# The experts' scatter as fp32r matmuls of a high and a low part

## The reference

```python
def moe_swiglu(h, w_router, w1, w3, w2):
    ...
    combine = jnp.sum(jax.nn.one_hot(top_idx, N_EXPERTS, dtype=jnp.float32)
                      * gate[..., None], axis=1)
    y = jnp.zeros(xt.shape, jnp.float32)
    for e in range(N_EXPERTS):
        y = y + combine[:, e:e + 1] * swiglu(xt, w1[e], w3[e], w2[e]).astype(jnp.float32)
```

## Time and profile before

| | us |
|---|---|
| median of 3 runs (1304.88 to 1309.19) | 1306.67 |
| the profiled execution, its own time | 1308.46 |
| its span, first to last instruction | 1306.3 |

### The profile page before, as it was taken

How to read it: one execution, slowest core, us unless ns; L and a number is a source line. 1 busy time by engine, 2 the same in 40 slices (tenths; PEclk the granted TensorE clock), 3 DMA queues, 4 the chain that set the end, 5 groups by cost and what they waited for, 6 DMA issues and landing times.

```text
span 1306.3 us, 29353 instructions
## 1 busy us (share of the span) xinstructions
PE 1275.3 (98%) x13943; PEld 723.1 (55%) x13943; DVE 314.3 (24%) x415; ACT 200.7 (15%) x278; POOL 50.4 (4%) x44
## 2 busy tenths in 40 slices
PE   8999999997999999999999999999999999999996
PEld 7888888896793355345335434533643553353354
DVE  5454444588431011010101101020110110100001
ACT  5344443354430000000000000000000000000001
POOL 2000000032010000000000000000000000000000
PEclk9999999997789999999999999999999999999998
DMA  9965555233167999999999999999999999999940
GB/s 347 393 213 189 183 181 189 95 118 131 56 226 295 394 409 403 386 406 411 388 398 414 384 402 410 413 397 387 415 390 401 409 405 386 399 411 395 381 188 34
DMA packets 97885, 419.04 MB, mean 321 GB/s; under 512 B 8585, under 2 KB 14770, under 8 KB 97762
## 3 DMA queue, kind: packets, MB, share of 16 engines
q1 hardware_dynamic: 94288, 410.59, 80.6%
q0 software_dynamic: 1808, 5.45, 1.6%
q10 hardware_dynamic: 1666, 1.10, 0.3%
HBM read 415.01 MB, written 2.10 MB: 319 GB/s over the span
## 4 chain that ended last, share of the span: by engine, by line
PE 93%; DVE 3%; ACT 1%; issue 1%; DMA 1%; POOL 0%; DVEq 0%; POOLq 0%
PE psum L670 44%; PE psum L681 22%; PE psum L589 7%; PE psum L591 7%; PE psum L590 7%; PE psum L597 2%; PE psum L661 2%; PE psum L786 1%; DVE rope_z L1319 1%; DVE low L1135 1%; PE psum L651 0%; PE psum L796 0%; PE psum L808 0%; DMA consts<-in_table 0%; ACT high L929 0%
## 5 line engine op out<-in xcount | busy, mean ns | idle before, releaser
L670 PE MATMUL psum<-up,xg 128*32 128x448 f32 x6144 | 580.2, 539 | 2.4 <-DVE xg L1216 2.4
L670 PEld LDWEIGHTS psum<-up,xg 128*32 128x32 f32 x6144 | 198.9, 110 | 376.2 <-issue 372.5
L681 PE MATMUL psum<-down,hid_t 128*32 128x256 f32 x5376 | 291.5, 379 | 0.0
L681 PEld LDWEIGHTS psum<-down,hid_t 128*32 128x32 f32 x5376 | 174.8, 110 | 117.9 <-issue 3.9
L1135 DVE TENSOR_TENSOR low<-raw,high 128x2048 fp32r<-128x2048 f32 x51 | 116.9, 2292 | 95.4 <-ACT high L929 95.3
L1255 DVE TENSOR_TENSOR sil<-sil,psum 128x1344 f32<-128x1344 f32 x16 | 24.9, 1554 | 472.3 <-PE psum L670 472.3
L929 ACT ACTIVATE high<-raw 128x2048 fp32r<-128x2048 f32 x51 | 97.9, 1919 | 91.8 <-PE psum L591 91.4
L589 PE MATMUL psum<-high,a_hi 128*128 128x512 f32 x256 | 99.9, 390 | 0.9 <-DVE a_lo L1173 0.9
L1230 DVE SCALAR_TENSOR_TENSOR x_res<-psum,smalls,x_res 128x1024 f32<-128x1024 f32 x16 | 19.8, 1280 | 332.6 <-PE psum L661 332.6
L591 PE MATMUL psum<-low,a_hi 128*128 128x512 f32 x256 | 99.7, 389 | 0.0
L590 PE MATMUL psum<-high,a_lo 128*128 128x512 f32 x256 | 99.6, 389 | 0.0
(11 more groups left out here) (144 smaller groups left out, 627.1 us busy)
## 6 DMA issues: line engine op xcount, KB each, us to landing
up<-in_moe_w SPq DMA_DIRECT2D x256, 896.0 KB, 8.0
down<-in_moe_w SPq DMA_DIRECT2D x112, 1024.0 KB, 7.9
raw<-in_ffn_w SPq DMA_DIRECT2D x42, 1024.0 KB, 5.2
raw<-in_w_q SPq DMA_DIRECT2D x4, 1024.0 KB, 5.2
raw<-in_w_o SPq DMA_DIRECT2D x4, 1024.0 KB, 4.9
x_res<-in_x SPq DMA_DIRECT2D x2, 512.0 KB, 4.7
raw<-in_pool_w SPq DMA_DIRECT2D x1, 1024.0 KB, 10.0
raw<-in_w_kv SPq DMA_DIRECT2D x1, 1024.0 KB, 5.2
```

Of the source, the lines that this page charges most:

```text
L670: mm = pe.matmul(out3[g * BLK:(g + 1) * BLK, r, :], xg[:, k, r * BLK:(r + 1) * BLK], w[:, g], start=k == 0, stop=k == DT - 1)
L681: mm = pe.matmul(Y[g * BLK:(g + 1) * BLK, r, :], hid_t[:, c, r, b * BLK:(b + 1) * BLK], w[:, bb, g * GW:(g + 1) * GW], start=c == 0 and b ...
```

## The change

y_sb becomes two tiles: y_hi, which ACT writes in fp32r, and y_lo, which DVE writes in fp32r as the difference between Y in PSUM and y_hi. pick_t becomes fp32r. In the scatter each block r is now multiplied twice, with y_hi for the four groups and then with y_lo for the four groups, into the same sums. The scatter waits for y_lo instead of y_sb. DVE's subtraction stands ahead of its wait for the scatter; for the last expert it stands ahead of the last addition.

```diff
@@ -206,8 +206,9 @@
         sil = at("sil", [P, NB, FG], F32, o_b)
         hid_t = at("hid_t", [P, MC, NB, FG], F32, o_b + NB * FG * 4)
         idx_dump = at("idx_dump", [P, NB, SEQ], F32, o_w)
-        pick_t = at("pick_t", [P, NB, SEQ], F32, o_w + 3 * K)
-        y_sb = at("y_sb", [P, NB, GW], F32, o_w + 16 * K)
+        pick_t = at("pick_t", [P, NB, SEQ], F32R, o_w + 3 * K)
+        y_hi = at("y_hi", [P, NB, GW], F32R, o_w + 16 * K)
+        y_lo = at("y_lo", [P, NB, GW], F32R, o_w + 8 * K)

         pooled_t = at("pooled_t", [P, DT, SEQ], F32, o_w)

...
@@ -656,10 +658,11 @@

                 for t in range(NT):
                     for r in range(NB):
-                        for g in range(4):
-                            q = slice(g * BLK, (g + 1) * BLK)
-                            mm = pe.matmul(scatter_out[:, g, t, :], pick_t[q, r, t * P:(t + 1) * P], y_sb[q, r, :],
-                                           start=r == 0, stop=r == NB - 1)
+                        for part in (y_hi, y_lo):
+                            for g in range(4):
+                                q = slice(g * BLK, (g + 1) * BLK)
+                                mm = pe.matmul(scatter_out[:, g, t, :], pick_t[q, r, t * P:(t + 1) * P], part[q, r, :],
+                                               start=r == 0 and part is y_hi, stop=r == NB - 1 and part is y_lo)
                 mm.then_inc(signal, 1)

             def expert_up(kind, c, k, out3):
...
@@ -687,7 +690,7 @@

             def scatter_previous(ps, e):

-                pe.wait_ge(y_ready, ps.experts(0, e))
+                pe.wait_ge(y_lo_ready, ps.experts(0, e))
                 pe.wait_ge(pick_t_ready, ps.experts(0, e))
                 scatter(scattered)

...
@@ -912,7 +915,7 @@
                 for ps in PASSES[1:]:
                     expert_pass(ps)
             keep_warm(0, 14)
-            pe.wait_ge(last_y, 1)
+            pe.wait_ge(last_lo, 1)
             scatter(last_scattered)


...
@@ -977,12 +980,12 @@

             def take_output(signal):

-                act.activation(y_sb[:], Y, ACT.Copy).then_inc(signal, 1)
+                act.activation(y_hi[:], Y, ACT.Copy).then_inc(signal, 1)

             def take_previous(ps, e):

                 act.wait_ge(unit_used, ps.units(0, e))
-                take_output(y_ready)
+                take_output(y_hi_ready)

             def expert_feed_forward(ps, e):
                 ps.later(act, e, take_previous)
...
@@ -1111,7 +1114,7 @@
             with act.If(again > 0):
                 for ps in PASSES[1:]:
                     expert_pass(ps)
-            take_output(last_y)
+            take_output(last_hi)


             norm(4, lambda t: (stream_done, t + 1), dump=squares)
...
@@ -1232,8 +1235,14 @@
                     if signals:
                         mm.then_inc(stream_done, 1)

+            def take_low(ready, n, signal):
+
+                dve.wait_ge(ready, n)
+                dve.tensor_tensor(y_lo[:], Y, y_hi[:].bitcast(F32), ALU.subtract).then_inc(signal, 1)
+
             def add_previous(ps, e):

+                take_low(y_hi_ready, ps.experts(0, e), y_lo_ready)
                 dve.wait_ge(scattered, ps.experts(0, e))
                 add_scattered(bass.ds(e, 1), False)

...
@@ -1472,6 +1481,7 @@
                     expert_pass(ps)


+            take_low(last_hi, 1, last_lo)
             dve.wait_ge(last_scattered, 1)
             add_scattered(slice(E, E + 1), True)
             dve.wait_ge(gf_in, 16)
```

More of the change, by code:

```diff
@@ L341, in trunk_program @@
         idx_summed, idx_ready, gathered, xg_ready = sem("idx_summed"), sem("idx_ready"), sem("gathered"), sem("xg_ready")
-        pick_t_ready, y_ready, scattered = sem("pick_t_ready"), sem("y_ready"), sem("scattered")
-        last_y, last_scattered = sem("last_y"), sem("last_scattered")
+        pick_t_ready, scattered = sem("pick_t_ready"), sem("scattered")
+        y_hi_ready, y_lo_ready = sem("y_hi_ready"), sem("y_lo_ready")
+        last_hi, last_lo, last_scattered = sem("last_hi"), sem("last_lo"), sem("last_scattered")
         dve_step, pool_step = sem("dve_step"), sem("pool_step")
```

## The result

The changed kernel takes 1294.97 us (median of 5 runs, 1293.63 to 1297.46), the kernel before 1304.88 us (median of 5, 1302.79 to 1309.19). The ratio is 0.992 with a 95% interval of 0.9905 to 0.9935: faster, by 6.5 to 9.5 in a thousand, clear of the 0.3% of measurement. 9.2 us less was forecast (1297.5 us, from the median of the first three runs); the medians of five differ by 9.9 us. The profiled execution took 1297.46 us, with a span of 1295.7 us, 10.6 us less than before.

What follows compares the result with a forecast made beforehand. TensorE was taken to bound the kernel; eight scatters, each shortened from 2.80 to 1.65 us, gain 8 x 1.15 = 9.2 us, so 1306.67 - 9.2 = 1297.5 us for the median, range 1293.5 to 1304 us.

Steps and rivals of the forecast that it cites:

- What bounds: Whole kernel: TensorE, busy 98% of the span, is the bound, so time taken from it is taken from the kernel.
- The step and the sum: Each scatter: 12 steps of 0.120 us plus 0.21 us exposed, 1.65 us instead of 2.80; eight gain 9.2 us.
- the rule: Scatter step: weight load takes columns over 1.2 in ns, 107 ns for 128 columns, whatever the rows.
- Beside TensorE: DVE's new subtraction before each scatter: 0.86 to 0.89 us, covered by 4.8 us of up projection; uncovered, 0.9 us each.
- A, no overlap in fp32r: Scatters: 32-row fp32r matmuls do not run beside each other, 48 steps, +3.17 us each, 1332 us; chance 8%.
- B, a rate of pairs: Scatters: rate of load-matmul pairs limits; no gain, 1306.7 us (7%), or floor per program matmul, 1327 us (3%).
- C, the clock at the end: Warming and last scatter: granted clock shifts; no fall gives 1294.4 us, low during scatter 1298.6 us; chance 17% together.
- C's first case: Warming matmuls before the last scatter: clock does not fall, 28 records take 3.1 us less, 1294.4 us.
- D, late weight loads: Expert weight loads: they run late and TensorE waits for them, so no change, 1306 us; chance 3%.

## Why the prediction was right

**What bounds.** TensorE is 93% of the chain that ended last in both profiles, and the time went where it was taken away:

```profile
PE psum L673 45%; PE psum L684 22%; PE psum L591 7%; PE psum L593 7%; PE psum L592 7%; PE psum L599 2%; PE psum L789 1%; PE psum L664 1%; DVE rope_z L1328 1%; DVE low L1138 1%; PE psum L653 0%; PE psum L799 0%; PE psum L811 0%; DMA consts<-in_table 0%; ACT high L932 0%
```

The scatter's line L664, 2% in the earlier trace rows, is at 1%.

**The step and the sum.** The forecast was 12 steps of 0.120 us and 0.21 us at the edges, 1.65 us, and it is 12 of 0.119 and 0.19, 1.62 us. The gain per scatter is 1.17 us for 1.15. All eight give 8.22 + 1.19 = 9.4 us for the 9.2 forecast, and the medians differ by 9.9 us in the first set and by 9.2 in the later one. That the split is paid for by the type was shown by the run in fp32, and that steps add up linearly by the run with the high part alone.

**Why 0.120.** Here the reasoning was only half right. It took the load of the weights as what holds a step, since 128 and 256 columns took about the same time at full height. The three runs on the step show load and stream level at 0.11 us: halving the weights does not help either. The number was right because it was read from a row with the same weights and the same columns, not from the rule.

**Beside TensorE.** The subtraction takes 0.958 us, more than the 0.86 to 0.89 that two longer instructions gave in proportion. Its cover of 4.8 us was as forecast, and the run with the scatter in front shows what the cover is worth: 2.0 us an expert for the copy and the subtraction together. The prediction had priced the subtraction alone, at 0.9.

**A, no overlap in fp32r.** Out: four groups start together. Its 1332 us supposed no overlap at all, and no run had that; the order by groups, meant to forbid it, still got a part and ended at 1308.44 us.

**B, a rate of pairs.** Out: 48 pairs in 1.62 us, and in 0.87 us when both sides are halved.

**C, the clock at the end.** It came in part. The clock did fall, but for 3.4 us where it had been 6.8, and that gave 1.20 us, less 0.28 us of a later start. That is the larger part of what the profiled executions differ by beyond the forecast (10.6 for 9.2 us; the rest is 0.3 us ahead of the experts and 0.2 us in the scatters). But no run shows that the change did it. The length of the low clock differs between traces, and C's first case, no fall at all, came in four traces of other kernels, where the warming took 3.32 us, 2.8 less than before for the 3.1 that C gave. Which case an execution falls into is chance as far as this record goes, so that the profiled execution gained more than the sum is luck. The prediction left open whether the warming was worth its time; it was not.

**D, late weight loads.** Out: the same 44.0 MB of an expert came in 110.19 us for 111.36, 1% faster, the loads landed after 8.0 us as before, and the periods are even: from 504.67 to 614.85 it is 110.18 us, and from there to 1165.79, five periods, 550.94 us, 110.19 each.

## What to carry to other kernels

Here an fp32 matmul of 32 rows became two fp32r matmuls on a high and a low part. A set of four groups takes two steps of 0.119 us for two of 0.216, a little over half as long, because the groups still run side by side. The other operand holds only ones and zeros; no run tried another one or measured the rounding. The split itself must have a place where another engine is idle and TensorE does not ask for it yet. Read the length of a step from a row that has both the same weight columns and the same streamed columns, since either can be what holds it. And when a stage has become short, look at the filler in front of it again: here it took 3.3 to 6.2 us, ahead of a last scatter that needs 1.75 us up to the addition at full clock and 3.0 us at half clock, and leaving it out gained some 4 us.

## What the hardware showed that was not expected

- TensorE does not start matmuls strictly in the order of the program. With six of one row group in a row, the next group's first started beside the third of them (3.34 us for 48 matmuls; a strict order would need at least 4.8 us, an estimate from steps of 0.119 us); with two in a row, all four groups started within 0.02 us.
- Load and stream are level for an fp32r matmul of 128 weight columns and 256 streamed ones: 0.119 us a step, 0.112 and 0.114 with one of them halved, 0.059 with both.
- The granted clock fell at one of seven idle places of 1.92 us, and cost 1.5 us there (periods of 113.27 and 112.61 us for 112.18).
- At the end, where TensorE is idle for 2.9 to 3.5 us ahead of the warming, the clock fell during the idle stretch or the warming in seven of the eleven traces with the warming and not in the other four; the same 28 records took 3.32 us without a fall and up to 6.15 us with one.
